# A two-layer encoder trunk on one core: Ada sums spread differently, head steps reordered, rotary parts by pairs of heads, gate copies on ScalarE

## The reference

```python
mod = silu(c) @ ada_w[i] + ada_b[i]          # six vectors of 2048: shift, scale, gate, twice
h = x * (1 + scale) + shift
x = layer_norm(alpha * x + (1 + gate) * y)   # y = mixer(h) or swiglu(h)
```

## Time and profile before

| | us |
|---|---|
| median of 3 runs | 2471.78 (2470.01 to 2475.72) |
| the profiled execution | 2477.09 |
| its span | 2475.4 |
| TensorE busy | 2247.9 |
| VectorE busy | 1584.7 |
| ScalarE busy | 984.2 |

### The profile page before, as it was taken

One profiled execution on the slowest core, in us unless ns is written; L12 is line 12 of the kernel. 1 busy time (PEld: TensorE's weight loads), 2 busy tenths in 40 slices (PEclk: granted clock), 3 DMA queues, 4 the chain that ended last, 5 costly groups with the idle time before them and its releaser, 6 DMA issues.

```text
span 2475.4 us, 25272 instructions
## 1 busy us (share of the span) xinstructions
PE 2247.9 (91%) x9976; PEld 1818.8 (73%) x9976; DVE 1584.7 (64%) x1782; ACT 984.2 (40%) x1274; POOL 104.0 (4%) x206
## 2 busy tenths in 40 slices
PE   4788887499999999999899999994999999999996
PEld 2376675388888888878677778783888888888885
DVE  5776677776766766667675555576766555455455
ACT  1155532344443344433343444433444433444432
POOL 2100001000000000000000000000000000000000
PEclk9998898699999999999899999996999999999998
DMA  9966668578786878777647766665778656566654
GB/s 392 414 244 226 224 227 321 197 264 292 280 286 218 285 295 284 283 282 251 250 157 245 239 230 236 195 247 195 255 280 274 189 171 193 194 191 189 190 187 145
DMA packets 136327, 601.27 MB, mean 243 GB/s; under 512 B 15504, under 2 KB 15760, under 8 KB 109968
## 3 DMA queue, kind: packets, MB, share of 16 engines
q1 hardware_dynamic: 108560, 398.31, 47.0%
q0 software_dynamic: 27648, 201.34, 22.3%
HBM read 597.49 MB, written 2.10 MB: 242 GB/s over the span
## 4 chain that ended last, share of the span: by engine, by line
PE 81%; DVE 8%; DMA 6%; ACT 2%; issue 2%; SPq 0%; ACTq 0%; DVEq 0%
PE ps L1195 50%; PE ps L1201 25%; DMA ada_head<-in_ada_w 3%; DMA ada_w<-in_ada_w 3%; DVE ada_w L756 2%; DVE wlo L737 1%; PE ps L1168 1%; PE ps L1304 1%; ACT whi L470 1%; DVE gate L756 1%; PE ps L1307 1%; PE ps L1312 1%; PE ps L1181 1%; DMA bf<-in_fox_b_f 1%; PE ps L1282 1%
## 5 line engine op out<-in xcount | busy, mean ns | idle before, releaser
L737 DVE TENSOR_TENSOR wlo<-raw,whi 128x1024 fp32r<-128x1024 f32 (+2 forms) x721 | 873.7, 1217 | 762.0 <-ACT whi L470 761.5
L470 ACT ACTIVATE whi<-raw 128x1024 fp32r<-128x1024 f32 (+2 forms) x721 | 758.4, 1054 | 1203.8 <-PE ps L1201 1137.7
L1195 PE MATMUL ps<-whi,hT_hi 128*128 128x512 f32 x1952 | 616.1, 397 | 1.0 <-DVE tmp L833 1.0
L1195 PE MATMUL ps<-whi,hT_lo 128*128 128x512 f32 x1952 | 607.9, 393 | 0.0
L1201 PE MATMUL ps<-wlo,hT_hi 128*128 128x512 f32 x1952 | 528.1, 393 | 17.9 <-DVE wlo L737 17.9
L1201 PEld LDWEIGHTS ps<-wlo,hT_hi 128*128 128x128 f32 x1952 | 369.1, 189 | 98.8 <-DVE wlo L737 21.7
L1195 PEld LDWEIGHTS ps<-whi,hT_lo 128*128 128x128 f32 x1952 | 370.2, 190 | 78.4
L1195 PEld LDWEIGHTS ps<-whi,hT_hi 128*128 128x128 f32 x1952 | 365.1, 190 | 78.5 <-issue 4.6
L756 DVE CUSTOM_DVE_ANT_0 ada_w<-ada_w,c_bc,cols 128x2048 f32<-128x2048 f32 x159 | 373.0, 2346 | 38.0 <-DMA ada_w<-in_ada_w 37.9
L1195 PE MATMUL ps<-whi,uT_lo 128*128 128x512 f32 x704 | 217.9, 391 | 0.0
L1195 PE MATMUL ps<-whi,uT_hi 128*128 128x512 f32 x704 | 217.9, 391 | 0.0
(11 more groups left out here) (198 smaller groups left out, 1345.1 us busy)
## 6 DMA issues: line engine op xcount, KB each, us to landing
raw<-in_ffn_w SPq DMA_DIRECT2D x528, 512.0 KB, 4.2
ada_w<-in_ada_w POOLq DMA_DIRECT2D x159, 1024.0 KB, 5.4
raw<-in_fox_w_in SPq DMA_DIRECT2D x96, 512.0 KB, 4.0
ada_head<-in_ada_w POOLq DMA_DIRECT2D x17, 1024.0 KB, 20.2
gate<-in_ada_w POOLq DMA_DIRECT2D x16, 1024.0 KB, 6.7
raw<-in_mla_w_o SPq DMA_DIRECT2D x32, 512.0 KB, 5.0
raw<-in_fox_w_o SPq DMA_DIRECT2D x32, 512.0 KB, 3.7
down_w<-in_mla_w_down SPq DMA_DIRECT2D x16, 544.0 KB, 8.0
```

The lines of the kernel that those rows point to most:

```text
L470: nc.scalar.activation(whi[:, s, 0:n], raw[:, s, 0:n], ACT.Copy).then_inc(hi_ready, 1)
L737: nc.vector.tensor_tensor(wlo[:, s, 0:n], raw[:, s, 0:n], whi[:, s, 0:n].bitcast(F32), ALU.subtract).then_inc(lo_ready, 1)
L1195: nc.tensor.matmul(ps[:, 2 * pair + t, 0:width], a[:, t * P:(t + 1) * P], w_hi, start=(first and c == 0 and a is hi), stop=False)
```

## The change

- **Ada sums.** Two further buffers, `ada_wide`, lie in the high and low halves of `hT` (heads 8 to 15), used for sums 32 to 53 in a round of five, from when the latent product is done. Sums in the program: four before the angles, four in the first projections, one at the start of each step of attention 0 and one after the mask in the first 17; four and two in the last blocks of `w_o(0)`; in the feed-forward one at every third unit, none in the last two units ahead of the u product; in FOX as before but only until sum 176.
- **Order on VectorE and ScalarE per head step.** The output's halves (`o_high`, `o_low`) are read at the start of the next step. `w_o` and the last block of a feed-forward do the residual before the next low part.
- **Rotary parts.** The columns of `mla_w_uq` and `mla_w_down` are laid out so that two heads' rotary parts fill one 128-row transpose; `kpT` holds the shared key twice, each with zeros in the other head's rows. One rotation serves both row tiles. The copy of `kpT` moves to ScalarE after projection 4, the scaling of xa too (steps 1 and 3).
- **Gate.** Its four parts go to four banks, in steps 16 to 18 of attention and at units 3 to 6 of the first w2 product; ScalarE copies them. `turn_u` moves from unit 1 to unit 2.
- **FOX.** The logits' transpose moves behind two units, the running sum into the middle of the projections; v's eviction is waited for only before v is read.
- **Loads.** `cols` has its own semaphore; SyncE holds the first raw loads until Ada sum 28; GpSimd issues seven Ada loads before the constants.

The diff, cut to its core:

```diff
+ADA_WIDE_UNTIL = 54
 def ada_slots():
         if n < ADA_HEAD:
             slots.append(n % 7)
+        elif n < ADA_WIDE_UNTIL:
+            slots.append((2, 0, 1, 7, 8)[(n - ADA_HEAD) % 5])
         elif n < ADA_GATE_UNTIL:
-            slots.append(n % 3)
+            slots.append((2, 0, 1)[(n - ADA_WIDE_UNTIL) % 3])
...
 def tick_gaps(layer, i):
-        return (1, 1, 0) if layer == 0 else (2, 2, 2)
-    return 1, 1, 0
+        return (1, 1, 0, 0) if layer == 0 else (2, 2, 2, 0)
+    if i < TICKS - 1:
+        return 1, 1, 0, 0
+    return 1, 0, 0, 1
+def gate_parts(i):
+    return {TICKS - 3: ((0, 4),), TICKS - 2: ((1, 5),), TICKS - 1: ((2, 6), (3, 4))}.get(i, ())
+    ada_wide = place_at("ada_wide", [P, 2, 2 * D], F32, a0)[:, :, D:2 * D]
...
+            sp.wait_ge(ada_done, ADA_HEAD - 4)
...
+            def gate_copy(part, bank):                        # ScalarE
+                act.wait_ge(gate_turned, pl.gate + 1)
+                nc.scalar.activation(gate[:, part * NB:(part + 1) * NB], ps[:, bank, :], ACT.Copy
+                                     ).then_inc(gate_copied, 1)
+                pl.gate += 1
+                def o_high(i):
+                    act.wait_ge(pv_done, H * layer + i + 1)
+                    if layer == 0 and i == H // 2:
+                        act.wait_ge(ada_done, ada_last(7))
+                    nc.scalar.activation(o_chunk(layer, i)[0], ps[:, 7, 0:S], ACT.Copy
+                                         ).then_inc(o_hi, 1)
+                    if i >= 4:
+                        o_high(i - 4)
...
-                    units(1)                                  # ScalarE, ffn
+                    units(2)
                     for b in range(2):
                         turn_plain(uT_hi, (nb - 1) * 4 + UC * b)
                     if n == 0:
-                        pl.turn += 4
-                    units(4 * 4 * nb // UC - 1)
+                        for part in range(4):
+                            gate_copy(part, 6 + part % 2)
+                    units(4 * 4 * nb // UC - 2)
...
-            def units_with_ada(n, every):                     # VectorE
+            def units_with_ada(n, spare=0):
                 for k in range(n):
                     units(1)
-                    if k % every == every - 1:
+                    if pl.pe % 3 == 0 and k < n - spare:
                         ada()
...
                 for i in range(TICKS):                        # VectorE, attention
+                    if i >= 4:
+                        o_low(i - 4)
+                    if layer == 0 or pl.ada < ada_end(1, SH_F):
+                        ada()
                     gap(gaps[0])
...
-                    if layer == 0:
+                    if layer == 0 and i < TICKS - 2:
                         ada()
                     gap(gaps[1])
                     gap(gaps[2])
-                    if layer == 0 and i % 2 == 0:
-                        ada()
-                    if i >= 3:
...
             def w_o(layer):
-                gate_in()
-                units(1)
-                residual(0, True)
-                units(1)
-                residual(1, True)
+                pl.gate += 4
+                if layer == 0:
+                    dve.wait_ge(xa_scaled, T)
+                for b in range(2):
+                    pl.pe += 1
+                    residual(b, True)
+                    ahead()
                 for b in (2, 3):
-                    for k in range(PAIRS):
+                    for k in range(PAIRS - (b == 3)):
                         units(1)
-                        if layer == 0 or k % 4 == 3:
+                        if layer == 0 and k in ((1, 3, 5, 7), (1, 3))[b - 2]:
                             ada()
+                    if b == 3:
+                        pl.pe += 1
                     residual(b, True)
...
             for k in range(MLA_GROUP):                        # VectorE
+                if k % 2 == 1:
+                    ada()
                 units(1)
-                if k in (1, 3):
-                    ada()
-                if k in (4, 6):
-                    scale_xa((k - 4) // 2, None)
...
+                    if rotary and i < H and i % 2 == 0:       # TensorE, attention
+                        pe.wait_ge(q_roped, 2 + i // HG)
                         if i >= 4:
-                            pe.wait_ge(o_lo, g - 3)
+                            pe.wait_ge(o_lo, i - 3)
...
-                            if b == 0 and j == 1:             # TensorE, ffn
+                            if b == 0 and j == 2:
                                 turn_u()
                                 u_turned = pl.turn
-                                if n == 0:
-                                    gate_turns(l, G_F)
+                            if n == 0 and b == 0 and 3 <= j < 7:
+                                if j >= 5:
+                                    pe.wait_ge(gate_copied, pl.gate - 1)
+                                gate_turn(l, G_F, j - 3, 6 + (j - 3) % 2)
```

More of the change, by code:

```diff
@@ L101, in __init__ @@
     def __init__(self):
-        self.unit = self.pe = self.block = self.turn = self.turn_act = self.step = self.ada = 0
+        self.unit = self.pe = self.block = self.turn = self.turn_act = self.step = self.ada = self.gate = 0
 def pair_uses(block, pair):
@@ L421, in load_ada @@
                     pool.wait_ge(ada_done, ada_slot_free(n))
+                if ADA_SLOT[n] >= 7 and not ada_slot_free(n):
+                    pool.wait_ge(down_used, KC)
                 pool.dma_start(ada_buffer(n), A["ada_w"][l, q, c]).then_inc(ada_in[ADA_SLOT[n]], 16)
-            for n in range(4):
+            for n in range(7):
                 load_ada(n)
@@ L920, in rope_keys @@
             def rope_keys():
-                src = ps[:, 6:8, 0:ROPE].rearrange("p t (f two) -> p t f two", two=2)
-                dst = kpe[:, :, :].rearrange("p t (f two) -> p t f two", two=2)
+                x0, x1 = (ps[:, 6:8, n * RH:(n + 1) * RH] for n in range(2))
                 parts = [rope_t[:, n, 0:T * RH].rearrange("p (t f) -> p t f", t=T) for n in range(4)]
-                t0, t1, t2, t3 = rope(src[:, :, :, 0], src[:, :, :, 1], cos[:, :, :], sin[:, :, :],
-                                      *parts)
@@ L927, in rope_keys @@
[L927 to L943 removed]
+                t0, t1, t2, t3 = rope(x0, x1, cos[:, :, 0, :], sin[:, :, 0, :], *parts)
@@ L967, in gap, with o_low @@
                         done[0] += 1
-                        if layer == 1 and done[0] % 4 == 0:
-                            ada()
+                def o_low(i):
+                    dve.wait_ge(o_hi, H * layer + i + 1)
+                    if layer == 0 and i == H // 2:
+                        dve.wait_ge(ada_done, ada_last(8))
+                    hi, lo = o_chunk(layer, i)
+                    nc.vector.tensor_tensor(lo, ps[:, 7, 0:S], hi.bitcast(F32), ALU.subtract
+                                            ).then_inc(o_lo, 1)
                 for i in range(TICKS):
@@ L1110, in _ @@
             nc.vector.tensor_copy(f_row[:, :], ps[0:H, 6, 0:S]).then_inc(f_done, 1)
+            for k in range(PAIRS, FOX_F + 1):
+                units(1)
+                proj_done(1, k)
             dve.wait_ge(turned, pl.turn + 1)
@@ L1258, in gap, with evicted @@
                         done[0] += 1
[L1260 to L1262 removed]
+                def evicted(h, n):
                     for pair in range(2):
[L1264 to L1266 removed]
+                        pe.wait_ge(pair_read[pair], pair_uses(first_block + h // HG * blocks + n, pair))
+                blocks = 4 if rotary else 3
                 first_block = pl.block - blocks
@@ L1336, in attention @@
                                          start=False, stop=True).then_inc(pv_done, 1)
+                    for part, bank in gate_parts(i):
+                        if part == 0:
+                            pe.wait_ge(qk_copied, H * (layer + 1))
+                        elif part == 1:
+                            pe.wait_ge(masked, H * (layer + 1))
+                        elif part == 2:
+                            pe.wait_ge(pT_copied, H * (layer + 1))
+                        else:
+                            pe.wait_ge(gate_copied, pl.gate - 2)
+                        gate_turn(layer, G_A, part, bank)
+                    gap(gaps[3])
             def w_o(layer):
-                gate_turns(layer, G_A)
                 out_product(layer, FIRST_OUT)
```

302 lines of the change are left out of this document (161 added, 141 removed).

## The result

| | before | after |
|---|---|---|
| median, us | 2473.75 (2470.01 to 2477.47, 4 runs) | 2342.64 (2338.56 to 2345.72, 4 runs) |
| the profiled execution | 2477.09 | 2345.72 |
| its span | 2475.4 | 2344.0 |

The ratio is 0.9469 (95% interval 0.9447 to 0.9491). The forecast was 2343, between 2312 and 2382.

What follows compares the result with a forecast made beforehand. The prediction took TensorE, busy in 91% of the span, as the bound, with only its idle time and low clock to win. Its terms summed to -128.2 us: 2477.1 becomes 2348.9, the median 2343.6; 2312 to 2382 holds 8 in 10.

Steps and rivals of the forecast that it cites:

- Attention 0: Attention 0 with its gate: from 202 us to 172, -30 us, with ends at 158 and 202.
- w_o(0) and norm 0: Output projection of layer 0 and its norm: from 107.3 us to 67, -40 us, with ends at 62 and 85.
- Feed-forwards and FOX: Feed-forward 0 -7.5 us, feed-forward 1 +2.6; FOX's start -14, its attention -4.5, its gate -1.
- The wait behind the gate copies: New TensorE idle of 1.9 us before unit 6 of the first second product in each feed-forward.
- the clock term behind it: Low clock behind the gate copies' wait in each feed-forward, bringing that wait's 1.9 us to 4.5.
- Norm 1: Norm behind feed-forward 0: a sum and two low parts moved from ahead of the residual, -2.3 us.
- head: Start of the kernel, 0 to 124 us, bound by the DMA engines: -1 us (0 to -4).
- Norm 2: Norm behind FOX: no sums left to do, its wait of 34.0 us becomes 8.5, -25.5 us.
- B: Rival, all fits: attention 0 at its content, w_o at 62, no idle at the gate copies; 2315 us, chance 0.12.
- C: Rival: moved sums wait for their rows in attention 0 (190 us) and w_o (85); 2379 us, chance 0.14.
- D: Rival: feed-forward 0 starves as raw loads land late, slower than before; 2501 us at 0.6 us per unit, chance 0.04.
- E: Rival: another wait takes the low part's place, perhaps the mask's, attention 0 stays at 198 us; 2369 us, chance 0.08.

Runs made afterwards that it cites:

- e11: The changed kernel with the rotary scores contracted over 64 rows, not 128 (half of the rotary term left out): 2348.38 us, ratio 0.9497 to the kernel before.
- e2: The changed kernel with the output's halves back at the end of their step, sums unchanged: 2339.42 us, ratio 0.9463 to the kernel before.
- b3: The kernel before, with only the Ada sum ahead of the low part in attention 0's even steps moved to the step's start: 2447.05 us, ratio 0.9897.
- e10: The kernel of e2 with each step's second Ada sum moved to right ahead of o_low: 2351.25 us, ratio 0.9503 to the kernel before.
- e1: The changed kernel without the two buffers in hT, sums 32 to 63 going round three buffers: 2343.56 us, ratio 0.9482 to the kernel before.
- e5: The changed kernel with the two rows of norms 0, 1 and 2 issued behind the next stage's first four weight loads: 2331.33 us, ratio 0.9436.
- e6: The changed kernel with Ada rows 37 to 79 loaded over 512 of 2048 columns, VectorE's instructions in full: 2329.39 us, ratio 0.9410 to the kernel before.
- b1: The kernel before, with only the Ada sums of its feed-forwards at every third unit, not every fourth: 2454.74 us, ratio 0.9907.
- e4: The changed kernel with ScalarE's casts of units 6 and 7 between gate copies in both feed-forwards: 2335.00 us, ratio 0.9454 to the kernel before.

## Why the prediction was right, point by point

The time was right, and so were the two largest terms. Their reasons are another matter, and for attention 0 the right number is in good part luck.

*Attention 0.* The forecast of 172 us was 158.5 of work and 14 for waits; it was 147.6 (144.9 and the unit), 16.5 of idle and 6.0 of clock. Three steps were off. The work was 11 us less, because I priced the pairing of rotary parts by the transposes that go (3 us) and not by what 64-row matmuls cost among 128-row ones (e11). The waits did not go: `o_low` at the head of the step stands on a VectorE that is nearly full (152.6 of 167.4 us), and five rotary transposes still wait for it. And the cause named first, the low part's place, adds nothing once the sums are out of its way (e2); the sum in front of it was what had stopped TensorE (b3, e10). The prediction had read that sum in the earlier trace rows, but it named both halves of the edit in one sentence and gave neither a share. It also had no term for the gate's wait and for the clock behind kpT's wait, 9 us together, nor for the new waits for the maximum and the probabilities, 6.1 us after 0.6. The work came out 11 us below the forecast and the waits with their clock 8.5 us above, and by luck these nearly cancel.

*w_o(0) and norm 0.* 68.1 against 67. The wait was forecast at 13 us and is 19.1; I had the two sums (4.7) and left out 6.2 us of late residual. The 5 us added for DMA covered most of it. The prediction was to be wrong if this wait stayed above 20 us; 19.1 is close to that, and e1, whose edit is elsewhere, has 20.1. The cause of a part of the late residual, two rows of a norm ahead of weights in SyncE's queue, is shown by e5; with Ada rows of a quarter of the bytes (e6), and the norm's two rows still ahead of the weights, the residual is only 0.5 us late, so the traffic of the Ada rows has its part in it. Buffers for the rows were not needed (e1). That the 39 us come from moving the sums out of this stage rests on the profiles and not on a run: VectorE's waits for rows there are 0.7 us, after 22.6 in the earlier trace rows, and TensorE's wait for the norm fell by 12.3 us.

*Feed-forwards and FOX.* The wait behind the gate copies is there, at 1.63 us for 1.9; the clock term behind it, 2.6 us in each, is what failed, and it makes half of the 5 us in feed-forward 1. A further 1.1 us there is an old wait that I had not booked, for uT_lo at the gate turns, and 0.3 the new wait's shorter length; 1.0 stays open. FOX comes out at -19.5 as forecast, but split otherwise: the slow stretch after the wait for cumT lies behind the first transposes, in the attention.

*Norm 1, head.* Norm 1's wait is 10.1 and not 8.5: its residual, too, waited for loads behind the norm's rows, 1.6 us (e5: 8.5). The head did not shorten: the first transposes of the latents begin 1.5 us later than before, and the way from there into attention 0 is 4.3 us shorter, for the 5 of kpT's wait. *Norm 2* fell by 25.5 in the change; b1 shows 23.2 of it from the denser sums alone.

*Rivals.* B is excluded in its terms for attention 0 and w_o. C is right that rows are waited for (10.3 us in six waits in attention 0, 0.7 in one behind it), not in the price; e6 shows that the landing matters as well. D had nothing for it in the changed kernel's feed-forward 0, which shortened by 9.0 us; b1 shows a trace of it. E, another wait in the place of the low part's, is half true: the low part's stayed, the one for the maximum behind the mask came (2.6 us), and yet the stage shortened.

## What to carry to other kernels

A sum of the right total can rest on wrong parts: when a change moves two instructions at once, move each alone before naming the one that paid. An operation that nobody waits for belongs behind the ones that somebody waits for in an engine's step, and bulk rows that are needed late belong behind the weights in the loading queue. And a matmul with fewer rows than its neighbours need not be a saving; padding it with zeros to their shape was one here.

## What the runs showed of the hardware

- Pairs of 64-row and 128-row matmuls of 256 columns took 463 and 449 ns each in a mean, pairs of 128-row ones 379 and 380, with the same columns and banks (e11, e4).
- The granted clock fell to 1.2 GHz behind some waits and not behind others of like length. In the changed kernel it stood at 0.52 in the seven us around a wait of 4.18 us at 243.76:

```profile
242.00:249.00 7.00, 5.24 (x16) 4.43 (x17) 6.96 (x14) 2.50 (x5) 1.06 (x2) 0.52 0.98 378
```

  It stood at 1.00 behind one of 1.63, and over the whole attention 0 of e4, with five waits of up to 3.2 us for the low part. In the kernel before, a wait of 1.62 us was enough:

```profile
251.32 0.41 PE L1291 MATMUL ps<-ident,mla_q 128*64 128x128 f32 x2 [1.62 <-DVE hT_lo L996]
```

```profile
252.50:260.00 7.50, 7.50 (x24) 6.25 (x24) 4.79 (x9) 3.03 (x6) 0.53 (x1) 0.54 0.85 285
```

  The length of a wait alone does not tell whether the clock falls. One profile of this stage can be 7 us off another with the same code; between the changed kernel and e4, 6.0 us of it are clock.
- The Trainium skill (page Trainium Kernel Development and Optimization, Key Constraints) says that the queues of SyncE and GpSimd share the DMA engines. These runs agree: with the bytes of GpSimd's rows at a quarter (e6) norm 0's wait falls by 6 us, and around w_o and norm 0 ScalarE's waits for SyncE's weights fall from 18.5 to 7.1 us.
